# A hybrid decoder trunk's mixer entry: x turned by products with its factors' diagonal, and a quarter of its squares moved to VectorE

## The chip, the cores and the metric

The kernel runs on one core of one Trainium2 chip. The metric is the device time of one execution in microseconds (us), as the median of the runs. A separate execution was recorded by the hardware profiler; its rows name the engines PE (TensorE matmul), PEld (TensorE weight load), DVE (VectorE), ACT (ScalarE), POOL (GpSimd) and SP (SyncE).

## The reference, cut to what matters

Two layers on x of 256 tokens by 2048 features, float32: a Mamba-2 mixer and an MLP, then a differential attention on shared keys and values and a second MLP. The change touches only the first lines of the first layer:

```python
def rms_norm(x, w, eps=NORM_EPS):
    xf = x.astype(jnp.float32)
    y = xf * lax.rsqrt(jnp.mean(xf * xf, axis=-1, keepdims=True) + eps)
    return (y * w.astype(jnp.float32)).astype(x.dtype)

# layer 0
u = rms_norm(h, norm_pre_mix[l])          # h is x
zxbcdt = u @ in_proj                      # 2048 -> 10304 features
```

So each token's row of x is multiplied by one factor, the inverse root of its mean square, then each feature by its weight, and the result goes into a product with `in_proj`.

## The kernel before

**Layout.** x lies in `h` as two token halves (t = 0, 1) of 128 rows by 2048 features. It is loaded in four quarters of 512 features (`piece(0)` to `piece(3)`), one DMA each for both halves, in the SP queue (L457). The products need x with its features on the partitions, so TensorE turns it: sixteen 128-feature tiles k, each for both halves, 32 turns of 128x128 in all. A "pair" i is the tiles 2i and 2i+1, that is four turns.

**Split numbers.** Every product with a weight matrix is made of three products of rounded parts: a value is high + low, and high x high, high x low and low x high are added. Weights arrive in slabs of 128x1024 (`raw`). ScalarE makes the high part (`split`, L664), VectorE the low part (`split`, L993). The turned x, multiplied by the norm's weight `par`, is split in the same manner: ScalarE makes `xhi` out of PSUM (L680), VectorE `xlo` (L1104).

**The entry.** What happens before the first product with a weight, in the order of the code:

- ScalarE squares and sums the eight blocks (four quarters, two halves) of x as they land (`square_sum`, L667: one pass of 128x512 with an accumulator, then a read of the accumulator), and counts each in the semaphore `h_sq`.
- TensorE runs unneeded transposes of the identity, `keep_awake` (L1779): ten when `h_sq` is 4, thirteen more when it is 6 (`FIRST_AWAKE`).
- When `h_sq` is 8, VectorE adds up the sums (L1039); ScalarE takes the root (L746) after it has copied the norm weights (L758); VectorE makes the factor `rsh` of each token (L1041 to L1049).
- x is multiplied by its factors into `y`: VectorE the first 512 features (L1275, four instructions of 128x256), ScalarE the other 1536 later (`scale_x`, L767, six of 128x512), placed between its splits.
- TensorE turns `y` against the identity (`transpose_scaled_x`, L1716), which waits for the `x_scaled` semaphore of its part. Pairs 0 and 1 come first, then four more `keep_awake` transposes, then slab 0's products in three groups of eight (`high_first`: L1729, L1735, L1738). Pairs 2 and 3 are turned inside slab 1's step, pairs 4 and 5 ahead of slab 3, pairs 6 and 7 ahead of slab 4. From slab 4 on, products run in threes (L1615, L1616, L1617); slab 5 is the time step's (L1684, L1685) and needs all of x.

Each engine takes its instructions in this written order, and semaphores hold them. `diagonal` (L1054) exists in the kernel for later norms: it writes the identity times the factors into `diag`, two 128x128 tiles, which TensorE multiplies by `ones` to spread the factors (L1785). The scratch `junk` receives the squares nobody reads.

Of the kernel before, what the change touches and what calls it, by code (L numbers as in the profile page):

```python
# [25 lines left out]
ALU = mybir.AluOpType  # L26
ACT = mybir.ActivationFunctionType
AX = mybir.AxisListType.X

P = 128  # L30
D = 2048
S = 256
MT = S // P
# [19 lines left out]
PIECES = 4  # L53
# [14 lines left out]
TURN_BANKS = (((3, 3), (4, 4), (5, 5), (6, 6), (2, 2), (7, 7), (3, 3), (4, 4)), MLP_TURNS,  # L68
              ((5, 7), (6, 6), (2, 2), (7, 7), (5, 5), (6, 6), (2, 2), (7, 7)), MLP_TURNS)
# [4 lines left out]
             (1, 0, 0, 512), (1, 1, 0, 512), (1, 2, 0, 512), (1, 3, 0, 256), (1, 3, 256, 512))  # L74
END_PART_BANKS = (0, 1, 2, 3, 4, 5, 6, 7, 0)
END_AWAKE = 14
X_PIECES = ((0, 256), (256, 512), (512, 1024), (1024, 1536), (1536, 2048))
X_PIECE = (0, 1, 2, 2, 3, 3, 4, 4)
H_PIECES = ((0, 128), (128, 256), (256, 512), (512, 1024), (1024, 1536), (1536, 2048))
H_PIECE = ((0, 1), (2, 2), (3, 3), (3, 3), (4, 4), (4, 4), (5, 5), (5, 5))  # L80
LAST_PARTS = ((0, 0, 512), (1, 0, 256), (1, 256, 512))
# [116 lines left out]
def piece(n):  # L198

    return slice(n * D // PIECES, (n + 1) * D // PIECES)  # L200

def build(nc, w, out):
# [47 lines left out]
    with ctx:  # L251
        def sb(name, shape, dt=F32, stack=ctx):
            return stack.enter_context(nc.sbuf_tensor(name, shape, dt))
# [15 lines left out]
        def sem(name):  # L269
            return ctx.enter_context(nc.semaphore(name))  # L270

        h = sb("h", [P, MT, D])
        y = sb("y", [P, MT, D])
# [16 lines left out]
        def raw_of(s):  # L290
# [6 lines left out]
        junk = sb("junk", [P, 2 * MT, BLK], BF16)  # L297
        ident = sb("ident", [P, P])
# [4 lines left out]
        diag = sb("diag", [P, MT, P])  # L303

        part = sb("part", [P, MT, NT + 2 + PIECES])
        ssy, ssh = part[:, :, 0:NT + 1], part[:, :, NT + 2:]
# [3 lines left out]
        sum_y, sum_h, rsy, rsh, ssg, rsg, rsa, rs_x, rs_h, rs_a, rs_k, root = (  # L310
            stat[:, 2 * i:2 * i + 2] for i in range(12))
        neglam = sb("neglam", [P, 4])
        rs_q = sb("rs_q", [P, MT])
        ps = ctx.enter_context(nc.psum_tensor("ps", [P, 8, BLK], F32))
# [67 lines left out]
        hi_ready, lo_ready, slab_used = sem("hi_ready"), sem("lo_ready"), sem("slab_used")  # L382
        consts_ready, small_in, norm_in = sem("consts_ready"), sem("small_in"), sem("norm_in")
        x_in = [sem(f"x_in{n}") for n in range(PIECES)]
        x_scaled = [sem(f"x_scaled{n}") for n in range(len(X_PIECES))]
        heads_in, rel_in, lam_in = sem("heads_in"), sem("rel_in"), sem("lam_in")
        par_t, par_ready = sem("par_t"), sem("par_ready")
        postw_in, cum_out, cumb_in, bias_out, tab_in = (
# [3 lines left out]
        y_sq, yw_ready, h_new, h_sq, rms_ready = sem("y_sq"), sem("yw_ready"), sem("h_new"), sem("h_sq"), sem("rms_ready")  # L392
# [260 lines left out]
        def _(act):  # L653
            chain = Tally(act, act_chain)
            sc = nc.scalar

            def split(s, lo=0):

                act.wait_ge(raw_in[s.raw], s.arrived)
                if isinstance(s.n, int) and s.n >= FIRST_HELD:  # L660
                    act.wait_ge(slab_used, s.n - 2 * LEAD + 1)
                elif above(s.n, LEAD - 1):
                    act.wait_ge(slab_used, s.n - LEAD + 1)
                sc.activation(slot_of(s, lo)[0], raw_of(s), ACT.Copy).then_inc(hi_ready, 1)  # L664

            def square_sum(slot, src, dst, done):
                sc.activation(junk[:, slot, 0:src.shape[-1]], src, ACT.Square, accum_out=dst).then_inc(done, 1)  # L667

            def h_squares(r, p):

                act.wait_ge(h_new, H_STEPS * (r - 1) + MT * (p + 3))
                if p >= 2:
                    act.wait_ge(h_sq, MT * PIECES * r + MT * (p - 1))
                for t in range(MT):
                    square_sum(MT * (p % 2) + t, h[:, t, piece(p)], ssh[:, t, p:p + 1], h_sq)
# [36 lines left out]
            def output_norm(ph, r, i):  # L712

                added = NT * (ph.block0 + ph.blocks - 1)
                if i == 1:
                    root_table()
                for nt in {2: (0,), 4: (1,), 6: (2,)}.get(i, ()):
                    act.wait_ge(acc_added, added + nt + 1)
                    for t in range(MT):  # L720
                        square_sum(MT * (nt % 2) + t, y[:, t, nt * BLK:(nt + 1) * BLK], ssy[:, t, nt:nt + 1], y_sq)
                if i < 7:
                    return
                for n, (t, lo, hi) in enumerate(LAST_PARTS):
                    if n < 2:
                        act.wait_ge(part_added, 2 * r + n + 1)
                    else:
                        act.wait_ge(acc_added, added + NT)
                    sc.activation(junk[:, MT + t, lo:hi], y[:, t, (NT - 1) * BLK + lo:(NT - 1) * BLK + hi], ACT.Square,
                                  accum_out=ssy[:, t, NT - 1 + n // 2:NT + n // 2]).then_inc(y_sq, 1)  # L730
                take_root(sum_y, r + 2)
# [19 lines left out]
            for p in range(PIECES):  # L751
                act.wait_ge(x_in[p], 16)
                if p >= 2:
                    act.wait_ge(h_sq, MT * (p - 1))
                for t in range(MT):
                    square_sum(MT * (p % 2) + t, h[:, t, piece(p)], ssh[:, t, p:p + 1], h_sq)
            act.wait_ge(par_t, 1)
            sc.activation(par[:, 0:32], ps[:, 2, 0:32], ACT.Copy).then_inc(par_ready, 1)  # L758
            take_root(sum_h, 1)
            act.wait_ge(par_ready, 1)  # L760

            def scale_x(n):

                lo, hi = X_PIECES[n]
                act.wait_ge(x_scaled[1], MT)
                for t in range(MT):
                    sc.activation(y[:, t, lo:hi], h[:, t, lo:hi], ACT.Copy, scale=rsh[:, t:t + 1]).then_inc(x_scaled[n], 1)  # L767

            split(mix.slab(0))
            x_halves(0, (0, 1), 0)  # L770
            split(mix.slab(1))
            scale_x(2)
            split(mix.slab(2))
            x_halves(0, (2, 3), 0)
            split(mix.slab(3))
            scale_x(3)
            scale_x(4)

            def first_step(unit, i):

# [204 lines left out]
        def _(dve):  # L985
            chain = Tally(dve, dve_chain)
            ve = nc.vector
# [48 lines left out]
            def inverse_by_root(dst, total, sums, count, halves=range(MT)):  # L1036

                ts = slice(halves[0], halves[-1] + 1)
                ve.reduce_sum(total[:, ts], sums[:, ts, :], AX).then_inc(summed, 1)  # L1039
                dve.wait_ge(summed, count)  # L1040
                chain.mark(ve.tensor_scalar(rs_h[:, ts], total[:, ts], -0.5 / D, None, ALU.mult))  # L1041
                dve.wait_ge(rooted, count)
                link(ve.reciprocal(rs_x[:, ts], root[:, ts]))
                for t in halves:
                    c = slice(t, t + 1)
                    chain.mark(ve.scalar_tensor_tensor(out=rs_a[:, c], in0=rs_x[:, c], scalar=rs_h[:, c], in1=rs_x[:, c],
                                                       op0=ALU.mult, op1=ALU.mult))
                chain.wait()
                link(ve.scalar_tensor_tensor(out=dst[:, ts], in0=rs_a[:, ts], scalar=1.5, in1=rs_x[:, ts], op0=ALU.add, op1=ALU.mult))  # L1049
# [217 lines left out]
            ve.memset(part[:, :, NT + 1:NT + 2], 1e-6 * D).then_inc(rows_cleared, 1)  # L1267
            ve.memset(par_rows[:, :, :], 0.0).then_inc(rows_cleared, 1)
            dve.wait_ge(rows_cleared, 1)
            dve.wait_ge(h_sq, MT * PIECES)  # L1270
            inverse_by_root(rsh, sum_h, ssh_and_eps, 1)
            for n in range(2):
                lo, hi = X_PIECES[n]
                for t in range(MT):
                    ve.tensor_scalar(y[:, t, lo:hi], h[:, t, lo:hi], rsh[:, t:t + 1], None, ALU.mult).then_inc(x_scaled[n], 1)  # L1275
            dve.wait_ge(par_ready, 1)
            split(mix.slab(0))
            x_halves(0, (0, 1), 0)
# [330 lines left out]
        def _(pe):  # L1609
            te = nc.tensor  # L1610
# [96 lines left out]

            def transpose_scaled_x(i):

                pe.wait_ge(x_scaled[X_PIECE[i]], MT)  # L1710
                if i >= 6:
                    pe.wait_ge(x_lo, i - 5)
                for j in range(2):
                    for t in range(MT):
                        k = 2 * i + j
                        last = te.transpose(ps[:, TURN_BANKS[0][i][j], j * S + t * P:j * S + (t + 1) * P], y[:, t, k * P:(k + 1) * P],  # L1716
                                            ident[:, :])
                last.then_inc(xt_done, 1)

            def high_first(s, i, turns=()):  # L1720
# [368 lines left out]
            for n, (bank, lo, hi) in enumerate(END_TURNED):  # L2089
                pe.wait_ge(end_weighed, 5 + n)  # L2090
                te.matmul(ps[:, bank, 0:hi - lo], diag[:, 1, :], y[:, 1, lo:hi], start=False, stop=True,
                          skip_group_check=True).then_inc(end_done, 1)
# [21 lines left out]
```

## Time and profile before

| what | value |
|---|---|
| median of 3 runs | 2521.24 us (2520.97 to 2521.31) |
| profiled execution, its own time | 2520.59 us |
| its span on the core | 2518.6 us |
| TensorE busy | 2504.8 us (99%) |
| VectorE busy | 1821.3 us (72%) |
| ScalarE busy | 1247.8 us (50%) |
| granted TensorE clock | 1.00 up to the last microseconds |

Times of rows are counted from the span's start; the span is 1.99 us shorter than that execution's time. A busy TensorE is not TensorE at its peak, since matmuls overlap: one of 128x128 is shown with some 0.27 us, but the next may start 0.11 us later. The chain of waits shows the second figure, the distance from one to the next, and that is what a further matmul costs.

### The profile page before, as it was taken

To read this page: it belongs to the slowest core of one execution; us is meant where nothing else is said; L and a number is where in the kernel's file an instruction comes from. 1 tells how busy PE (TensorE), PEld (TensorE's weight loads), DVE (VectorE), ACT (ScalarE), POOL (GpSimd) and SP (SyncE) were. 2 spreads that over 40 slices of the span, in tenths; PEclk is the share of its full clock that TensorE was granted. 3 is DMA by queue.
4 is the path that set the end of the run, shared out by engine and by line. 5 is a ranking of instruction groups with operands and counts; after the bars stand their busy time and mean duration, and the time that the engine had idled before them with its cause. 6 is when DMAs were issued, how large, how long until landed. Compare 5 with 4: busy or idle time off the path is not lost.

```text
span 2518.6 us, 42151 instructions
## 1 busy us (share of the span) xinstructions
PE 2504.8 (99%) x15444; PEld 2237.5 (89%) x15444; DVE 1821.3 (72%) x2572; ACT 1247.8 (50%) x1631; POOL 155.9 (6%) x271
## 2 busy tenths in 40 slices
PE   8999999999999999999999999999999999999999
PEld 8999999999898888888888998998898888888887
DVE  6877877787876675766667877778866667576667
ACT  7555545555654444444444754455644444444444
POOL 2222112211100000000000000000000000000000
PEclk9999999999999999999999999999999999999999
DMA  7666566656556666666666555555566666666664
GB/s 221 214 193 205 170 191 193 200 167 201 168 192 193 184 199 189 188 190 190 192 184 199 193 176 181 179 172 168 183 189 191 192 183 197 188 191 191 191 192 151
DMA packets 267240, 474.10 MB, mean 188 GB/s; under 512 B 16673, under 2 KB 50066, under 8 KB 265618
## 3 DMA queue, kind: packets, MB, share of 16 engines
q1 hardware_dynamic: 264194, 457.53, 59.4%
q0 software_dynamic: 2624, 15.00, 1.6%
q8 instruction: 55, 0.90, 0.2%
q10 hardware_dynamic: 336, 0.41, 0.0%
q14 instruction: 31, 0.25, 0.0%
HBM read 470.70 MB, written 2.19 MB: 188 GB/s over the span
## 4 chain that ended last, share of the span: by engine, by line
PE 99%; DVE 0%; DMA 0%; issue 0%; ACT 0%; SPq 0%; ACTq 0%; DVEq 0%
PE ps L1615 23%; PE ps L1617 23%; PE ps L1616 23%; PE ps L1644 16%; PE ps L1646 9%; PE ps L1877 1%; PE ps L1751 0%; PE ps L1975 0%; PE ps L1882 0%; PE ps L1810 0%; PE ps L1779 0%; DMA h<-x 0%; PE ps L2005 0%; PE ps L1729 0%; PE ps L1716 0%
## 5 line engine op out<-in xcount | busy, mean ns | idle before, releaser
L993 DVE TENSOR_TENSOR whl<-raw,whl 128x1024 fp32r<-128x1024 f32 x856 | 1062.4, 1241 | 591.5 <-ACT whl L664 578.7
L664 ACT ACTIVATE whl<-raw 128x1024 fp32r<-128x1024 f32 x856 | 906.8, 1059 | 1084.9 <-PE ps L1617 733.8
L1644 PE MATMUL ps<-xhl,whl 128*128 128x512 f32 x1792 | 623.0, 390 | 0.0
L1646 PE MATMUL ps<-xhl,whl 128*128 128x256 f32 x1792 | 505.3, 282 | 0.0
L1615 PE MATMUL ps<-whl,bhl 128*128 128x512 f32 x1284 | 500.5, 390 | 0.0
L1617 PE MATMUL ps<-whl,bhl 128*128 128x512 f32 x1284 | 499.2, 389 | 0.0
L1616 PE MATMUL ps<-whl,bhl 128*128 128x512 f32 x1284 | 499.1, 389 | 0.0
L1615 PE MATMUL ps<-xhl,whl 128*128 128x256 f32 x1748 | 493.5, 282 | 0.0
L1616 PE MATMUL ps<-xhl,whl 128*128 128x256 f32 x1748 | 488.1, 279 | 0.0
L1617 PE MATMUL ps<-xhl,whl 128*128 128x256 f32 x1748 | 487.6, 279 | 0.0
L1644 PEld LDWEIGHTS ps<-xhl,whl 128*128 128x128 f32 x1792 | 336.4, 188 | 71.1
L1646 PEld LDWEIGHTS ps<-xhl,whl 128*128 128x128 f32 x1792 | 338.6, 189 | 1.1
L1615 PEld LDWEIGHTS ps<-xhl,whl 128*128 128x128 f32 x1748 | 328.6, 188 | 0.5
L1616 PEld LDWEIGHTS ps<-xhl,whl 128*128 128x128 f32 x1748 | 328.8, 188 | 0.1
L1617 PEld LDWEIGHTS ps<-xhl,whl 128*128 128x128 f32 x1748 | 328.5, 188 | 0.0
L1615 PEld LDWEIGHTS ps<-whl,bhl 128*128 128x128 f32 x1284 | 241.0, 188 | 54.0 <-issue 4.8
L1617 PEld LDWEIGHTS ps<-whl,bhl 128*128 128x128 f32 x1284 | 241.1, 188 | 50.1
L1616 PEld LDWEIGHTS ps<-whl,bhl 128*128 128x128 f32 x1284 | 241.2, 188 | 47.8
L1093 DVE TENSOR_TENSOR y<-y,ps 128x1024 f32<-128x1024 f32 x138 | 168.4, 1220 | 5.1 <-PE ps L1617 0.8
L1615 PE MATMUL ps<-khl,whl 128*128 128x256 f32 x256 | 72.6, 284 | 0.0
L1617 PE MATMUL ps<-khl,whl 128*128 128x256 f32 x256 | 71.5, 279 | 0.0
L1616 PE MATMUL ps<-khl,whl 128*128 128x256 f32 x256 | 71.5, 279 | 0.0
(268 smaller groups left out, 2082.0 us busy)
## 6 DMA issues: line engine op xcount, KB each, us to landing
raw<-mlp_w SPq DMA_DIRECT2D x512, 512.0 KB, 4.2
raw<-a_in_proj SPq DMA_DIRECT2D x161, 512.0 KB, 4.6
raw<-a_out_proj SPq DMA_DIRECT2D x64, 512.0 KB, 4.1
raw<-b_w_q SPq DMA_DIRECT2D x32, 512.0 KB, 4.2
raw<-w_k SPq DMA_DIRECT2D x32, 512.0 KB, 4.1
raw<-w_v SPq DMA_DIRECT2D x32, 512.0 KB, 3.7
raw<-b_out_proj SPq DMA_DIRECT2D x32, 512.0 KB, 3.7
cumb<-cum_scratch POOLq DMA_DIRECT2D x8, 1024.0 KB, 7.2
```

The lines of the kernel that those rows point to most:

```text
L664: sc.activation(slot_of(s, lo)[0], raw_of(s), ACT.Copy).then_inc(hi_ready, 1)
L993: ve.tensor_tensor(out=low, in0=raw_of(s), in1=hi.bitcast(F32), op=ALU.subtract).then_inc(lo_ready, 1)
L1093: ve.tensor_tensor(out=cols, in0=cols, in1=ps[:, bank:bank + 2, :], op=ALU.add).then_inc(acc_added, 1)
L1615: te.matmul(outs, lh, rh, start=start, stop=False, skip_group_check=True)
L1616: te.matmul(outs, lh, rl, start=False, stop=False, skip_group_check=True)
L1617: return te.matmul(outs, ll, rh, start=False, stop=stop, skip_group_check=True)
L1644: te.matmul(ps[:, f, :].rearrange("p (q n) -> p q n", q=2), wh[:, j, c], xboth[:, :, k, :], start=k == 0, stop=False, skip_group_check=True)
L1646: last = te.matmul(ps[:, f, 0:S], wl[:, j, c], xhi[:, k, :], start=False, stop=k == KT - 1, skip_group_check=True)
L1877: te.matmul(ps[r % 2 * PD:(r % 2 + 1) * PD, 5 + r // 4, col:col + P], xd[:, c, r * PD:(r + 1) * PD], m[:, c, r, :], start=True, stop=True, ...
```

## The change

- The scaling of x goes away on both engines (L767 and L1275), with its semaphores `x_scaled`.
- In its place VectorE writes the factors on a diagonal with `diagonal(rsh, x_diag)`, two instructions of 128x128.
- TensorE turns unscaled x: the block of `h` is the stationary operand, `diag[:, t, :]` the moving one, so that the product is the turned block times the factors. It is an ordinary float32 `matmul`, no longer a `transpose`. All 32 wait for one semaphore, `x_diag`.
- The squares of the second token half of quarters 2 and 3 go from ScalarE to VectorE (`tensor_tensor_reduce`). ScalarE's one remaining square of each of these quarters counts two in `h_sq`.

```diff
-            def square_sum(slot, src, dst, done):
-                sc.activation(junk[:, slot, 0:src.shape[-1]], src, ACT.Square, accum_out=dst).then_inc(done, 1)
+            def square_sum(slot, src, dst, done, counts=1):
+                sc.activation(junk[:, slot, 0:src.shape[-1]], src, ACT.Square, accum_out=dst).then_inc(done, counts)
...
-                for t in range(MT):
-                    square_sum(MT * (p % 2) + t, h[:, t, piece(p)], ssh[:, t, p:p + 1], h_sq)
+                for t in range(MT if p < 2 else 1):
+                    square_sum(MT * (p % 2) + t, h[:, t, piece(p)], ssh[:, t, p:p + 1], h_sq, 1 if p < 2 else MT)
...
-            def scale_x(n):
-
-                lo, hi = X_PIECES[n]
-                act.wait_ge(x_scaled[1], MT)
-                for t in range(MT):
-                    sc.activation(y[:, t, lo:hi], h[:, t, lo:hi], ACT.Copy, scale=rsh[:, t:t + 1]).then_inc(x_scaled[n], 1)
-
             split(mix.slab(0))
             x_halves(0, (0, 1), 0)
             split(mix.slab(1))
-            scale_x(2)
             split(mix.slab(2))
             x_halves(0, (2, 3), 0)
             split(mix.slab(3))
-            scale_x(3)
-            scale_x(4)
...
             dve.wait_ge(rows_cleared, 1)
+            for p in range(2, PIECES):
+                dve.wait_ge(x_in[p], 16)
+                dve.wait_ge(h_sq, MT * (p - 1))
+                chain.mark(ve.tensor_tensor_reduce(
+                    out=junk[:, MT * (p % 2) + 1, :], in0=h[:, 1, piece(p)], in1=h[:, 1, piece(p)], scale=1.0, scalar=0.0,
+                    op0=ALU.mult, op1=ALU.add, accum_out=ssh[:, 1, p:p + 1]))
+            chain.wait()
             dve.wait_ge(h_sq, MT * PIECES)
             inverse_by_root(rsh, sum_h, ssh_and_eps, 1)
-            for n in range(2):
-                lo, hi = X_PIECES[n]
-                for t in range(MT):
-                    ve.tensor_scalar(y[:, t, lo:hi], h[:, t, lo:hi], rsh[:, t:t + 1], None, ALU.mult).then_inc(x_scaled[n], 1)
+            diagonal(rsh, x_diag)
...
             def transpose_scaled_x(i):
 
-                pe.wait_ge(x_scaled[X_PIECE[i]], MT)
+                if i == 0:
+                    pe.wait_ge(x_diag, MT)
                 if i >= 6:
                     pe.wait_ge(x_lo, i - 5)
                 for j in range(2):
                     for t in range(MT):
                         k = 2 * i + j
-                        last = te.transpose(ps[:, TURN_BANKS[0][i][j], j * S + t * P:j * S + (t + 1) * P], y[:, t, k * P:(k + 1) * P],
-                                            ident[:, :])
+                        last = te.matmul(ps[:, TURN_BANKS[0][i][j], j * S + t * P:j * S + (t + 1) * P], h[:, t, k * P:(k + 1) * P],
+                                         diag[:, t, :], start=True, stop=True, skip_group_check=True)
                 last.then_inc(xt_done, 1)
```

The order of instructions at the places that matter. TensorE, from the first fillers (`ident` alone is a `keep_awake` transpose) to slab 0's first products, before:

```order
L1779 MATMUL ps<-ident 128x128 x9
L1779 MATMUL ps<-ident 128x128 [waits h_sq]
L1779 MATMUL ps<-ident 128x128 x12
L1716 MATMUL ps<-ident,y 128x128 [waits x_scaled0]
L1716 MATMUL ps<-ident,y 128x128 x3
L1716 MATMUL ps<-ident,y 128x128 [waits x_scaled1]
L1716 MATMUL ps<-ident,y 128x128 x3
L1779 MATMUL ps<-ident 128x128 x4
L1729 MATMUL ps<-xhl,whl 128x256 [waits x_hi,hi_ready]
```

The same stretch of TensorE after, where lines of this part of the file have numbers 7 lower:

```order
L1772 MATMUL ps<-ident 128x128 x12
L1709 MATMUL ps<-diag,h 128x128 [waits x_diag]
L1709 MATMUL ps<-diag,h 128x128 x7
L1772 MATMUL ps<-ident 128x128 x4
L1722 MATMUL ps<-xhl,whl 128x256 [waits x_hi,hi_ready]
```

The eight turns stay where they were, between the 23 fillers and the four; two waits have become one. The order counts instructions of the program, one for each product, whatever it is on the engine.

VectorE, from the cleared rows to slab 0's low part, before (`stat` holds the sums, the root and the factors):

```order
L1268 MEMSET par_rows 128x512
L1039 TENSOR_REDUCE stat<-part 128x2 [waits h_sq,rows_cleared]
L1041 TENSOR_SCALAR stat<-stat 128x2 [waits summed]
L1043 RECIPROCAL stat<-stat 128x2 [waits rooted]
L1046 SCALAR_TENSOR_TENSOR stat<-stat 128x1 [waits dve_chain]
L1046 SCALAR_TENSOR_TENSOR stat<-stat 128x1
L1049 SCALAR_TENSOR_TENSOR stat<-stat 128x2 [waits dve_chain]
L1275 TENSOR_SCALAR y<-h,stat 128x256 [waits dve_chain]
L1275 TENSOR_SCALAR y<-h,stat 128x256 x3
L993 TENSOR_TENSOR whl<-raw,whl 128x1024 [waits hi_ready,par_ready]
```

The same stretch after, with line numbers 12 lower behind the squares:

```order
L1256 MEMSET par_rows 128x512
L1261 ISA junk,part<-h 128x512 [waits h_sq,x_in2,rows_cleared]
L1261 ISA part 128x1
L1261 ISA junk,part<-h 128x512 [waits h_sq,x_in3]
L1261 ISA part 128x1
L1027 TENSOR_REDUCE stat<-part 128x2 [waits h_sq,dve_chain]
L1029 TENSOR_SCALAR stat<-stat 128x2 [waits summed]
L1031 RECIPROCAL stat<-stat 128x2 [waits rooted]
L1037 SCALAR_TENSOR_TENSOR stat<-stat 128x2 [waits dve_chain]
L1042 TENSOR_SCALAR diag<-ident,stat 128x128 [waits dve_chain]
L1042 TENSOR_SCALAR diag<-ident,stat 128x128
L981 TENSOR_TENSOR whl<-raw,whl 128x1024 [waits hi_ready,par_ready]
```

Each square on VectorE is two instructions (the pass and the read of its sum), and both stand ahead of the first sum of sums. The four scalings have become two writes of the diagonal.

## Rows read from the trace of the kernel before

**Rows 1.** The page: busy time of each engine.

```profile
PE 2504.8 (99%) x15444; PEld 2237.5 (89%) x15444; DVE 1821.3 (72%) x2572; ACT 1247.8 (50%) x1631; POOL 155.9 (6%) x271
```

**Rows 2.** Stretches: from:to and length us, TensorE busy (records), granted clock, DMA share, GB/s.

```profile
8.43:12.82 4.39, 4.38 (x23) 1.00 1.06 401
13.18:31.00 17.82, 17.76 (x151) 1.00 0.84 206
31.00:60.00 29.00, 29.00 (x252) 1.00 0.64 194
...
100.00:2505.00 2405.00, 2403.72 (x14610) 1.00 0.61 187
```

**Rows 3.** The chain of waits, first 16 us: start us, us, what.

```profile
1.95 6.52 DMA h<-x
...
9.85 1.34 ACT junk L667 x4
...
11.29 0.17 DVE stat L1039
...
12.51 0.19 DVE y L1275
12.70 0.08 issue
12.77 0.36 DVE y L1275
13.13 0.04 issue
13.18 1.18 PE ps L1716 x8
14.36 0.44 PE ps L1779 x4
14.79 0.06 issue
14.85 1.18 PE ps L1729 x8
```

**Rows 4.** The queries on x: issue of quarters 2 and 3, and their landing.

```profile
L457 SPq DMA_DIRECT2D h<-x x2: 463/502/541, 2.0 to 2.5; - x2
...
DMA to landing us min/median/max: 6.5/6.9/7.4
```

**Rows 5.** Timeline, entry: start us, us, engine, line, operation [idle before, releaser].

```profile
9.85 0.63 ACT L667 ACTIVATE junk<-h 128x512 bf16<-128x512 f32 x1
...
10.39 0.18 ACT L667 ACTIVATION_READ_ACCUMULATOR junk<-h 128x1 f32 x1
...
13.87 1.57 ACT L680 ACTIVATE xhl<-ps,par 128x256 fp32r<-128x256 f32 x4 [1.23 <-PE ps L1716]
```

**Rows 6.** Timeline of TensorE's fillers, from 8 and from 12.5 us.

```profile
8.43 3.46 PE L1779 MATMUL ps<-ident 128*128 128x128 f32 x15 [1.18 <-ACT junk L667]
...
12.32 0.49 PE L1779 MATMUL ps<-ident 128*128 128x128 f32 x3
```

**Rows 7.** Instruction groups with forms kept apart: xcount, busy us, mean ns, idle before.

```profile
L1716 PE MATMUL ps<-ident,y 128*128 128x128 f32 x32 | 4.3, 276 | 0.4 <-DVE y L1275 0.4
L1785 PE MATMUL ps<-diag,ones 128*128 128x128 f32 x12 | 1.8, 274 | 0.0
L1054 DVE TENSOR_SCALAR diag<-ident,stat 128x128 f32<-128x128 f32 x6 | 3.0, 540 | 0.0
L1450 DVE SCALAR_TENSOR_TENSOR relu<-relu,rs_row 128x512 f32<-128x512 f32 x56 | 36.2, 688 | 1.0
L1161 DVE SCALAR_TENSOR_TENSOR h<-y,stat,h 128x512 f32<-128x512 f32 x18 | 12.7, 745 | 0.1
L1049 DVE SCALAR_TENSOR_TENSOR stat<-stat 128x2 f32<-128x2 f32 x4 | 0.6, 160 | 0.1
```

**Rows 8.** The chain of waits at three later places.

```profile
24.38 0.87 PE ps L1716 x8
...
82.47 1.09 PE ps L1882 x8
...
729.15 0.44 PE ps L1785 x4
```

**Rows 9.** The diagonals of later norms: count, ns min/median/max.

```profile
L1054 DVE TENSOR_SCALAR diag<-ident,stat x6: 278/285/1057, 722.6 to 1832.0; 128x128 f32<-128x128 f32 x6
```

More of the change, by code:

```diff
@@ L76 @@
 END_AWAKE = 14
-X_PIECES = ((0, 256), (256, 512), (512, 1024), (1024, 1536), (1536, 2048))
-X_PIECE = (0, 1, 2, 2, 3, 3, 4, 4)
 H_PIECES = ((0, 128), (128, 256), (256, 512), (512, 1024), (1024, 1536), (1536, 2048))
@@ L384, in build @@
         x_in = [sem(f"x_in{n}") for n in range(PIECES)]
-        x_scaled = [sem(f"x_scaled{n}") for n in range(len(X_PIECES))]
+        x_diag = sem("x_diag")
         heads_in, rel_in, lam_in = sem("heads_in"), sem("rel_in"), sem("lam_in")
```

## The prediction

> **What bounds the kernel now.** I read the page's busy line first: TensorE is busy for 2504.8 of 2518.6 us, and no other engine is above three quarters [rows 1]. So the 13.8 us in which it isn't busy are looked for next, in the stretches: from 31 to 60 us it is busy all the time, and in the 2405 us from 100 on it lacks 1.28 us [rows 2]. What is left lies ahead of the first products, and in the tail, which the change doesn't touch. Two rules follow. Whatever is added to TensorE's own queue behind the entry is paid in full. Whatever is taken from ScalarE or VectorE behind the entry is worth nothing, because they don't hold TensorE there.
>
> The entry itself is read in the chain of waits [rows 3]: x's third quarter lands at 8.47, ScalarE squares until 11.19, the factors take until 12.5, two scalings of VectorE until 13.13, and TensorE turns from 13.18, fills with four transposes, and starts slab 0's products at 14.85. From there the chain is TensorE alone. So the question is when the products with slab 0 start, and how much is added behind.
>
> **The squares.** ScalarE's four passes between x's third quarter, at 8.5, and 11.19 become two [rows 3]. But the last quarter bounds the gain: it was issued at 2.5 and took 7.4 us to land, so it is there at about 9.9 [rows 4]. ScalarE's last remaining square can't start earlier than the one that starts at 9.85 now, and its accumulator is read by 10.39 + 0.18 = 10.57 [rows 5]. VectorE's square has no row here. Its nearest are passes of 128x512 over two float32 operands, 0.688 to 0.745 us, and 0.16 us for an operation on one or two columns, as the read of the sum is [rows 7]. With 0.70 + 0.16, less some overlap, from 9.9 it ends at 10.7, and the sum of sums starts at about 10.8, where it started at 11.29 [rows 3]. Gain: 0.5 us, not the 1.3 us that ScalarE sheds. Bounds: nothing gained below the landing (ScalarE's 10.57, so at best 0.6 us), and on the other side a pass at half that rate, below.
>
> **The diagonal.** Before, the first scaling started 12.51 - 11.29 = 1.22 us behind the sum of sums, and the second ended 0.62 us later [rows 3]. Now the first diagonal write starts at 10.8 + 1.22 = 12.02. Two writes of 128x128, 0.28 us each in most of the six rows there are and 0.2 us apart, end at 12.4. The longest of the six took 1.06 us [rows 9]; that is the upper bound, and would make it 13.3. I take 0.28, the median.
>
> **What the earlier factors meet.** TensorE is not free at 12.4. Its 23 fillers start at 8.43, when ScalarE has squared quarter 1, which the change leaves where it is. Fifteen of them are (3.46 - 0.48) / 14 = 0.213 us apart, the last ones 0.11 us, and the last starts at 12.54 [rows 6], so the next instruction can start at 12.65. The second group of fillers waits for `h_sq` of 6, which is reached earlier now, but the first ten last until 8.43 + 10 x 0.213 = 10.56 anyway, so nothing moves. The turns start at 12.65 instead of 13.18: 0.53 us.
>
> **The turns.** This is the term that decides. A turn was a transpose: 32 in the program, 32 records, eight in 0.87 us, 0.109 each [rows 7, 8]. Now it is a float32 product. The kernel has the like: `spread_rs` multiplies `ones` by `diag`, two products for each of three norms, six in all, and the trace has twelve records of them, four in 0.44 us [rows 7, 8]. So a float32 product of 128x128 is two records of 0.11, and a turn goes from 0.109 to 0.218 us. A dearer neighbour is L1882 (four products for a group, eight records): 1.09 us, 0.136 each, with waits in it [rows 8]. I take 0.109, since the nearest shape is the diagonal's own.
>
> - Pairs 0 and 1: 8 x 0.218 = 1.74, from 12.65 to 14.39; then four fillers, 0.44, to 14.83; slab 0's products follow at 14.85 to 14.9. That is the time they start at now. Is the other input there? ScalarE starts on the turned pair 0.69 us behind the first turn, and needs some 0.8 us for two tiles [rows 5]; a pair takes 0.44 us longer now, so 12.65 + 1.13 + 0.8 = 14.6. Yes, just. VectorE, free from 12.4 and with two writes for four scalings, has slab 0's low part earlier. So the 0.53 us gained ahead of the turns are spent in them: net zero.
> - Pairs 2 to 7: 24 turns stand between products in a queue without gaps, so each costs its whole 0.109 more: 24 x 0.109 = 2.6 us. Their readers have room: ScalarE's and VectorE's parts of pair 7 take under 3 us behind the last turn, (four tiles take ScalarE 1.57 us [rows 5]), beside slab 4's 24 products at the 29.0 / 252 = 0.115 us of a record in rows 2, 2.8 us, and slab 5, which needs them, comes after.
>
> **The scalings.** ScalarE loses six passes and VectorE four. Nothing waited for ScalarE's, and by the first rule this is worth nothing. It is cover, though, for ScalarE's part of the turned x and slab 4's split, which come earlier against TensorE. No queue of SP or POOL is passed by anything.
>
> **The sum.** 0 at the start, +2.6 behind it. The profiled span goes from 2518.6 to 2521.2, its time from 2520.59 to 2523.2; against the median of the runs, 2521.24, that is 2523.9 us, 0.10% more. A measurement of this kernel can tell about 0.2%, 5.0 us, from no change, so the call is "the same", with a leaning to slower. Up to 1.3 us of it could be taken up by the short gaps behind 100 us [rows 2]; at the dearer 0.136 the 48 records of pairs 2 to 7 cost 6.5 us where the 24 transposes cost 2.6, so +3.9: 2525.1.
>
> **Rivals.**
>
> - *VectorE comes late.* If its square takes twice the 0.69 us of the nearest pass, 1.38, the first one runs from 8.5 past 9.9, the second to 11.3, with the read 11.45, behind ScalarE's end of today. Then the diagonal is there at 13.1, and everything is 0.45 us later: 2524.4. A diagonal write of 1.06 us gives 0.65 us in its own right, both together 1.3: up to 2525.2. For it: neither has a clean row in the entry. Against it: every pass of two float32 operands in rows 7 runs at the single rate. Chance 0.14. The Trainium skill (Vector Engine (DVE) Microarchitecture Reference, Points that are easy to get wrong) says that a scalar-tensor-tensor shape with two sources in SBUF that aren't bf16 runs at half throughput, no port being left for the accumulator. By that rule the rival would hold for the square; rows 7 disagree for the same shape without an accumulator (L1161, 745 ns), and no row shows one with it.
> - *The other side: a product is four records.* Slower than before by more than 0.2%. If TensorE took a real float32 product against a data block in four records, a turn would cost 0.436: pairs 0 and 1 end at 12.65 + 3.49 = 16.14, slab 0 starts at 16.6, 1.75 late, and the others add 24 x 0.327 = 7.85: 2530.8. It decides from three records a turn on: 24 x 2 x 0.109 + 0.9 = 6.1 us, beyond 5. Against it: twelve records for six products [rows 7]. Chance 0.04. The Trainium skill (TensorE: Matmul & The Clock Gate, Terms) names the transpose mode as four times faster for FP32; by that rule this rival would be the result. The trace says two.
> - *A turn stays one record.* If the product cost what the transpose did, pairs 0 and 1 would be done at 13.52, ScalarE's first tiles at about 14.15, and slab 0 would start 0.65 us earlier: 2520.6. Against it stand the same twelve records. Chance 0.04.
> - *The change doesn't bring its factors earlier*, because the last quarter lands late and the fillers end late. That is part of the forecast for the half it is true.
>
> **How the numbers follow.** Forecast, with its small variations, 0.74: 2523.9. VectorE late 0.14: 2524.4 to 2525.2. Four records 0.04, one record 0.04, and 0.04 for something in the placement of the program that rows don't show, either side. The first two hold 0.88, so the range goes from the forecast less the gaps' 1.3 and the run's own spread, 2522.0, to the dearer price on top with a late diagonal, 2526.0. Above 2526.3 (slower by over 0.2%) lie the four-record case and half of the rest: 0.06. Faster by over 0.2% would need 5 us from an entry in which 0.65 is the most that I find: 0.01. The same: 0.93.
>
> **What the changed profile would show.** The turns as 64 records, eight products (16 records) in 1.74 us in the chain; if there are 32 or 128, the sum fails. The sum of sums at 10.8 (11.45: half rate). The first turn at 12.65 with the last filler just ahead of it; if it starts at 13.1 or later with "DVE diag" as its releaser, VectorE is late. Slab 0's first product between 14.8 and 15.0. ScalarE idle more from 16 to 28 us, TensorE without a gap there, and its products from slab 4 on starting 2.6 us later than now. The forecast is wrong if a gap opens ahead of slab 4 or 5, or if the span from the first product on changes by other than 2.6 us.

## The result

| | before | changed |
|---|---|---|
| median | 2521.10 us (2520.79 to 2522.17, 22 runs) | 2524.27 us (2523.77 to 2525.59, 22 runs) |
| profiled execution's span | 2518.6 us | 2522.1 us |
| median span of those runs | 2519.1 us | 2522.35 us |

The ratio is 1.0012, with a 95% interval of 1.0007 to 1.0018: 3.2 us more, inside the 0.2% that count as no change here, and with the sign that the sum gave. The forecast was 2523.9, so 2.7 or 2.8 us more. The 3.5 us between the two profiled spans is a little too much: the span of before in its profile is 0.5 us shorter than its median span. Where this lies is said below.

### The profile page after: what moved, and what is told of

It is laid out like the page before. It is cut to its first block, busy times and chain, and to the rows that moved or that the text cites. A ratio compares the mean times of both kernels' runs of the same rounds, so it can differ in the third digit from the quotient of the medians.

```text
span 2522.1 us, 42207 instructions
## 1 busy us (share of the span) xinstructions
PE 2508.2 (99%) x15476; PEld 2241.0 (89%) x15476; DVE 1823.0 (72%) x2574; ACT 1243.7 (49%) x1621; POOL 156.4 (6%) x271
## 4 chain that ended last, share of the span: by engine, by line
PE 98%; DVE 1%; DMA 0%; ACT 0%; issue 0%; SPq 0%; ACTq 0%; DVEq 0%
PE ps L1607 23%; PE ps L1609 23%; PE ps L1608 23%; PE ps L1636 16%; PE ps L1638 9%; PE ps L1870 1%; PE ps L1744 0%; DVE whl L981 0%; PE ps L1968 0%; PE ps L1875 0%; PE ps L1803 0%; PE ps L1709 0%; DMA h<-x 0%; PE ps L1772 0%; DVE y L1081 0%
```

## The profile after

Line numbers are those of the changed kernel: 7 lower for TensorE, 12 for VectorE, 2 for ScalarE. First the page's busy line, which answers to [rows 1]:

```profile
PE 2508.2 (99%) x15476; PEld 2241.0 (89%) x15476; DVE 1823.0 (72%) x2574; ACT 1243.7 (49%) x1621; POOL 156.4 (6%) x271
```

TensorE has 15476 - 15444 = 32 records and 3.4 us of busy time more; ScalarE is 4.1 us less busy. Where the records are, by the query on the line of the turns (count, ns min/median/max, first and last start):

```profile
L1709 PEld LDWEIGHTS ps<-diag,h x64: 186/192/193, 12.9 to 31.6; 128*128 128x128 f32 x64
L1709 PE MATMUL ps<-diag,h x64: 270/275/377, 12.9 to 31.7; 128*128 128x128 f32 x64
```

32 turns are 64 records where they were 32 in [rows 7]. Now the chain of waits, to be laid beside [rows 3] (start us, us, what):

```profile
2.46 7.23 DMA h<-x
...
10.31 0.73 ACT junk L665 x2
...
11.14 0.18 DVE stat L1027
...
12.36 0.55 DVE diag L1042 x2
...
12.95 2.05 PE ps L1709 x16
15.00 0.44 PE ps L1772 x4
15.44 0.93 PE ps L1722 x8
...
19.17 1.78 PE ps L1709 x16
...
25.63 1.79 PE ps L1709 x16
...
30.21 1.78 PE ps L1709 x16
```

Two things are to be seen. Behind the first product with a weight each group of eight turns takes 1.78 or 1.79 us where it took 0.87: 5.35 - 2.61 = 2.74 us in three groups. One of the three groups of before is in [rows 8]; the other two are:

```profile
18.83 0.87 PE ps L1716 x8
...
28.07 0.87 PE ps L1716 x8
```

Ahead of it, slab 0's products start later. How much has to be read from the timelines of TensorE. The chain gives an instruction that waited its real start (14.85 before), but one that followed another on the same engine the modelled end of that other (15.44 now). The real starts, before and then now:

```profile
14.19 0.60 PE L1779 MATMUL ps<-ident 128*128 128x128 f32 x4
14.85 1.18 PE L1729 MATMUL ps<-xhl,whl 128*128 128x256 f32 x8
```

```profile
12.95 2.05 PE L1709 MATMUL ps<-diag,h 128*128 128x128 f32 x16 [0.69 <-DVE diag L1042]
14.84 0.60 PE L1772 MATMUL ps<-ident 128*128 128x128 f32 x4
15.19 1.18 PE L1722 MATMUL ps<-xhl,whl 128*128 128x256 f32 x8
```

So slab 0's products start 15.19 - 14.85 = 0.34 us late, where the forecast had zero. The turns started 0.23 us earlier than before (12.95 against 13.18), they took 1.89 us instead of 1.01 up to the first of the four fillers, and from there to the products it is 0.35 us instead of 0.66, since TensorE waited there before.

The sum of sums was only 0.15 us earlier than before (11.14 against 11.29), since the last quarter landed later in this execution. Its landing can be read off VectorE's square, for which everything else was done by 9.7:

```profile
10.27 0.69 DVE L1261 CUSTOM_DVE_ANT_0 junk<-h 128x512 bf16<-128x512 f32 x1 [0.54 <-DMA h<-x]
10.31 0.63 ACT L665 ACTIVATE junk<-h 128x512 bf16<-128x512 f32 x1 [0.63 <-issue]
...
10.88 0.08 DVE L1261 DVE_READ_ACCUMULATOR2_ANT part<- 128x1 f32 x1
```

It landed at some 10.3 us, against 9.9 in [rows 4]. (The chain's row for x ends at 9.69, where ScalarE had finished its square before; the query on x's transfers gives up to 7.8 us from issue to landing, and 2.46 + 7.8 is 10.3.) The square takes 0.69 us and the read of its sum 0.08. From landing to the sum of sums it is 0.85 us now; before, ScalarE alone took from 9.85 to 11.29, 1.44 us. So that part is worth its 0.6 us at this place. Behind the entry TensorE is as busy as before: 2403.7 us of the 2405 from 100 us on (2403.72 before, 2403.65 after).

```profile
100.00:2505.00 2405.00, 2403.65 (x14620) 1.00 0.61 187
```

The start and the turns make 0.34 + 2.74 = 3.1 us of the 3.5 between the two profiled spans. The rest need not be the change's. From slab 0's first product to the end, the execution of before took 2518.6 - 14.85 = 2503.8 us. Five other profiles below that also have single transposes behind the first pairs took 2504.0 to 2504.4, and those with products for all turns 2506.7 to 2507.1. The profile of before is the shortest of its kind by 0.2 to 0.6 us.

## The experiments

All medians are of 11 executions, each beside the kernel before on the same chip (33 executions). The intervals of the ratios are all about 0.09% wide to either side, that is 2.3 us. They separate the group at 3 us from zero, but not differences of a few tenths, which I read from the medians and from the profiles together and call indications.

### One part alone: the squares

```diff
-                for t in range(MT):
-                    square_sum(MT * (p % 2) + t, h[:, t, piece(p)], ssh[:, t, p:p + 1], h_sq)
+                for t in range(MT if p < 2 else 1):
+                    square_sum(MT * (p % 2) + t, h[:, t, piece(p)], ssh[:, t, p:p + 1], h_sq, 1 if p < 2 else MT)
...
+            for p in range(2, PIECES):
...
+                chain.mark(ve.tensor_tensor_reduce(
```

> The kernel before with the squares' part of the change alone: VectorE squares the second token half of quarters 2 and 3, the scaling of x and the transposes stay. My theory (the squares' part brings the factors half a microsecond earlier, TensorE's added records cost the rest): about 0.45 us faster than before, 2520.65 us, with the first turn some 0.45 us earlier than in a before whose last quarter lands at the same time. Rival (the fillers or the landing hold the turns whatever the squares do): no change, 2521.1 us. Rival (the squares on VectorE cost time): over 2521.3 us.

Measured: 2520.95 us against 2521.20, ratio 0.9998 (0.9989 to 1.0007). Not to be told from no change, and half of the 0.45 us expected. Its profile shows why the other half may be missing. The fillers, the factors' last scalings and the turns (timeline):

```profile
8.44 5.12 PE L1786 MATMUL ps<-ident 128*128 128x128 f32 x23 [1.18 <-ACT junk L667]
...
12.38 1.14 DVE L1282 TENSOR_SCALAR y<-h,stat 128x256 f32<-128x256 f32 x4
13.40 1.04 PE L1723 MATMUL ps<-ident,y 128*128 128x128 f32 x8
```

The second of the four scalings ends at about 13.0, but the turns start at 13.40: the 23 fillers took 5.12 us, all 0.213 us apart, where those of before took 4.38 (the first fifteen 0.213 apart, the last ones 0.11 [rows 6]). Here the fillers hold the turns.

### One part undone: the squares back on ScalarE

```diff
-                for t in range(MT if p < 2 else 1):
-                    square_sum(MT * (p % 2) + t, h[:, t, piece(p)], ssh[:, t, p:p + 1], h_sq, 1 if p < 2 else MT)
+                for t in range(MT):
+                    square_sum(MT * (p % 2) + t, h[:, t, piece(p)], ssh[:, t, p:p + 1], h_sq)
...
-            for p in range(2, PIECES):
...
-                chain.mark(ve.tensor_tensor_reduce(
```

> The changed kernel with all eight squares back on ScalarE, so that only the diagonal and the products are left of the change. My theory: the 24 later turns cost 2.7 us, the first eight 0.9 us less what the two shorter writes of the diagonal give back (0.2 us): about 3.4 to 3.6 us slower than before, 2524.6 us, so 0.3 to 0.45 us slower than the changed kernel. Rival (the squares on VectorE are a cost of the change and not a gain): as fast as the changed kernel or faster, 2524.3 us or less.

Measured: 2524.06 us against 2521.20, ratio 1.0011 (1.0002 to 1.0020). The loss is here without the squares' part. But it is 2.9 us, less than the 3.4 to 3.6 expected. So it was run once more, in a later job beside the changed kernel:

> The changed kernel with the squares back on ScalarE, once more, on one chip with the changed kernel. My theory of the forecast (the squares' part gains half a microsecond ahead of the turns): 0.3 us or more slower than the changed kernel. Theory after the first job (inside the change the squares' part gains nothing, since the fillers, whose end varies, and not the factors let TensorE go): within 0.15 us of it.

> The changed kernel itself once more, on the chip of this job, as the measure for the others: 3.0 us slower than before, 2524.2 us.

Measured: products only 2523.81, changed 2524.01, before 2521.06 us (ratios 1.0011, 1.0002 to 1.0020; and 1.0012, 1.0003 to 1.0021). The squares' part, which alone gave an indication of 0.25 us, shows no gain inside the change. Two things can be seen behind it. One is the fillers again; the chains of the two profiles, products only and then the changed kernel:

```profile
8.50 5.17 PE ps L1765 x23
13.67 1.95 PE ps L1702 x16
```

```profile
8.38 4.84 PE ps L1772 x23
13.22 1.79 PE ps L1709 x16
```

In both the chain goes from the fillers straight to the turns; neither the squares nor the diagonal are in it. In the changed kernel the second write of the diagonal had ended at 12.10 + 0.54 = 12.64, and the turns started behind the last filler, at 13.05 in the timeline. This isn't so in every execution. In the first profiles of the same two programs both chains go through the squares and the diagonal: the turns start at 13.37 with products only and at 12.95 in the changed kernel, though x's last quarter was squared from 10.16 in the one and from 10.31 in the other. There the squares' part did bring the turns forward. How often it does, no run counts; the median spans say little on average. The other is outside the span: the median span is 2522.2 us for products only and 2522.1 for the changed kernel, but the execution's time is 1.64 us longer than the span for products only, 1.92 for the changed kernel and 1.97 for before. In the first job it was 1.62 as well, and the changed kernel with early fillers, below, has 1.78. Why the time around the span differs between programs isn't known; no row shows it.

### The later turns as transposes again

```diff
-                        last = te.matmul(ps[:, TURN_BANKS[0][i][j], j * S + t * P:j * S + (t + 1) * P], h[:, t, k * P:(k + 1) * P],
-                                         diag[:, t, :], start=True, stop=True, skip_group_check=True)
+                        dst, c = ps[:, TURN_BANKS[0][i][j], j * S + t * P:j * S + (t + 1) * P], slice(k * P, (k + 1) * P)
+                        if i < 2:
+                            last = te.matmul(dst, h[:, t, c], diag[:, t, :], start=True, stop=True, skip_group_check=True)
+                        else:
+                            last = te.transpose(dst, y[:, t, c], ident[:, :])
```

ScalarE's `scale_x` comes back with it, and waits for `x_diag`.

> The changed kernel for the squares, the diagonal and pairs 0 and 1, but ScalarE scales the other 1536 features of x again and pairs 2 to 7 are transposes of the scaled x, as before. My theory (24 products of two records each cost 24 x 0.11 us more than 24 transposes): 2.65 to 2.75 us faster than the changed kernel, 2521.6 us, so 0.3 to 0.6 us slower than before. Rival (the loss comes from the entry, where TensorE waits for the diagonal): at most 0.5 us faster than the changed kernel, 2523.8 us or more.

Measured: 2521.52 us against 2521.20, ratio 1.0002 (0.9993 to 1.0011). All but 0.3 us of the loss is gone (2.75 us against the changed kernel's 2524.27), with the squares, the diagonal and the first eight products still in. From the chain:

```profile
18.96 0.87 PE ps L1728 x8
...
24.51 0.87 PE ps L1728 x8
...
28.19 0.87 PE ps L1728 x8
```

The three groups are back at 0.87 us. The loss sits in pairs 2 to 7, and ScalarE's six scalings beside them cost nothing.

### Records without products

Before, with each of these 24 transposes issued twice into the same place:

```diff
-                        last = te.transpose(ps[:, TURN_BANKS[0][i][j], j * S + t * P:j * S + (t + 1) * P], y[:, t, k * P:(k + 1) * P],
-                                            ident[:, :])
+                        for again in range(1 if i < 2 else 2):
+                            last = te.transpose(ps[:, TURN_BANKS[0][i][j], j * S + t * P:j * S + (t + 1) * P],
+                                                y[:, t, k * P:(k + 1) * P], ident[:, :])
```

> The kernel before, with each of the 24 transposes of pairs 2 to 7 issued twice into the same place; nothing else of the change. My theory (what the change costs is the number of records in TensorE's queue behind the first product, whatever they compute): 24 x 0.11 = 2.6 us slower than before, 2523.8 us. Rival (a record of a float32 product is dearer than a transpose, or the loss is elsewhere): clearly less than the 2.85 us by which the transposes from pair 2 on were faster than the changed kernel, under 2 us. Rival (TensorE's queue has room here): no change.

Measured: 2523.88 us against 2521.03, ratio 1.0010 (1.0001 to 1.0019): 2.85 us. From the chain:

```profile
19.64 1.75 PE ps L1717 x16
...
26.06 1.75 PE ps L1717 x16
```

Sixteen transposes take 1.75 us, sixteen records of products 1.78. So what is paid is a record's place in TensorE's queue; that it is a product and not a transpose makes 0.03 us for sixteen. Within what the medians can tell this is the change's whole later loss, without a diagonal, without a float32 product and without any of its other parts.

### The four fillers between turns and products

```diff
-AWAKE, FIRST_AWAKE = 24, (10, 13, 4)
+AWAKE, FIRST_AWAKE = 24, (10, 13, 0)
```

> The changed kernel without the four unneeded transposes between the first turns and slab 0's products. My theory: in the changed kernel's profile these products start straight behind the fillers (15.19 behind 14.84 plus 0.44), and ScalarE's first two tiles of the turned x are ready at about 15.0, so 0.2 to 0.3 us is gained: 2524.0 us. Rival (ScalarE's tiles end the wait by themselves and the fillers lie beside it): no change, 2524.3 us.

Measured: 2524.21 us against 2521.20, ratio 1.0011 (1.0002 to 1.0020): 3.01 us more than before, where the changed kernel has 3.17 and 2.95. These medians can't tell my 0.2 to 0.3 us from nothing. The profile speaks for the rival, no change. Timeline:

```profile
14.30 2.03 PE L1709 MATMUL ps<-diag,h 128*128 128x128 f32 x16
...
15.47 1.73 ACT L678 ACTIVATE xhl<-ps,par 128x256 fp32r<-128x256 f32 x4 [1.42 <-PE ps L1709]
...
16.46 0.71 PE L1722 MATMUL ps<-xhl,whl 128*128 128x256 f32 x4
```

ScalarE's first two tiles, 0.8 to 0.9 us from 15.47, end at 16.3, and the product starts at 16.46 without fillers in between. From the first turn to the product it is 2.16 us, against 2.24 and 2.15 in the two profiles of the changed kernel. Turns and fillers together only just cover these tiles; when the fillers go, the tiles are the wait.

### The fillers ahead of the turns: earlier, or fewer

Seven more fillers, begun when `h_sq` is 2 (squares-only, changed and before with this alone):

```diff
+            pe.wait_ge(h_sq, MT)
+            keep_awake(7, 0)
             for n in range(2):
```

> The squares-only kernel with seven more fillers, started two squares earlier (at about 6.8 us instead of 8.4). My theory (in many executions the fillers still run 0.21 us apart when the factors are there, so that they and not the factors let TensorE go at 13.3; TensorE comes up to its full rate the earlier the earlier it is kept busy): fillers end before 12.5, the first turn follows VectorE's second scaling, 0.2 us faster than squares-only, 2520.7 us. Rival (the fillers don't hold the turns): the same as squares-only, 2520.95 us. Rival (seven more transposes are just work in the way): slower than squares-only.

> The changed kernel with the same seven early fillers. My theory: 0.2 to 0.4 us faster than the changed kernel (2524.2), the first turn starting straight behind the second write of the diagonal, and still 2.7 us slower than the squares-only kernel with early fillers. Rival (the diagonal, not the fillers, holds the turns in most executions): no change, 2524.2 us.

> The kernel before with the seven early fillers alone. My theory: its factors come late enough for the fillers to be done in most executions, so at most 0.1 us faster than before, 2521.1 us. Rival (the fillers hold the kernel before as well): 0.2 us or more faster, as much as the early fillers give the squares-only kernel.

Measured against 2521.03: 2520.90 (0.9999, 0.9990 to 1.0008), 2523.92 (1.0011, 1.0002 to 1.0020) and 2521.12 (1.0000, 0.9991 to 1.0009). None differs from its kernel without these fillers by more than the measurement can tell. The mechanism that I had put behind the first two is refuted by the profiles. The fillers of squares-only, of changed and of before:

```profile
7.09 6.37 PE L1786 MATMUL ps<-ident 128*128 128x128 f32 x30
```

```profile
7.08 6.30 PE L1772 MATMUL ps<-ident 128*128 128x128 f32 x30
```

```profile
7.13 6.29 PE L1779 MATMUL ps<-ident 128*128 128x128 f32 x30
```

Thirty at 0.213 us are 29 x 0.213 + 0.27 = 6.4 us: nearly all ran at the wide spacing, although TensorE had been kept busy 1.3 us longer. Being busy earlier didn't bring the narrow spacing forward (it came at 13.0, 12.9 and 12.9), and the additional fillers ended no sooner: turns at 13.30, 13.22 and 13.41.

Five fillers less:

```diff
-AWAKE, FIRST_AWAKE = 24, (10, 13, 4)
+AWAKE, FIRST_AWAKE = 24, (10, 8, 4)
```

> The squares-only kernel with five fillers less ahead of the turns (18 for 23). In the profiles so far TensorE went over from 0.21 to 0.11 us a filler between 11.1 and 14.4 us, whatever time they began at. My theory (the fillers' end holds the turns where that comes late): at 0.213 us each the 18 end at 12.3, the turns start with the factors at 12.7, 0.2 to 0.3 us faster than squares-only, 2520.7 us. Rival (the gap ahead of the turns, or turns that run at the slower spacing, give it back): 2520.95 us or more.

> The changed kernel with five fillers less ahead of the turns. My theory: where the fillers' end holds the turns, 0.2 to 0.4 us faster than the changed kernel of the same job. Rival (16 records at the slower spacing, 0.21 us each, take longer than the fillers did): the same or up to 0.5 us slower.

Measured against 2521.06: squares-only 2520.69 us (0.9999, 0.9990 to 1.0008), changed 2523.94 (1.0013, 1.0004 to 1.0022). Squares-only with 18 fillers has the lowest median of all kernels here, 0.37 us below before, where 23 fillers gave 0.25; the changed kernel gains 0.07 at most, which is nothing. The timeline of the first:

```profile
8.23 3.53 PE L1786 MATMUL ps<-ident 128*128 128x128 f32 x18 [1.16 <-ACT junk L667]
...
12.97 1.18 PE L1723 MATMUL ps<-ident,y 128*128 128x128 f32 x8 [1.21 <-DVE y L1282]
```

TensorE is idle for 1.21 us ahead of the turns, and they run at the narrow spacing all the same. The direction agrees with the fillers as the holder, and the size is too small to be shown. This profile doesn't show it either: the narrow spacing came at 11.0 in it, as early as in the changed kernel's first profile, where all 23 fillers were through by 12.1. No version beats before by more than the measurement can tell.

## Why the prediction was right, point by point

- **TensorE is the bound; behind the entry its queue is paid in full.** Held. 24 idle transposes cost 2.85 us, 24 second records of the changed kernel 2.74 us in the chain. The 1.3 us of gaps behind 100 us took up nothing; they were there unchanged.
- **A turn becomes two records.** Held: 64. The term was 24 x 0.109 = 2.6; it measured 2.74 in the chain, because sixteen records of products take 1.78 us, 0.111 each, and not 1.74. The rivals of four records and of one are refuted by the count. The rule of the Trainium skill (TensorE: Matmul & The Clock Gate, Terms), a transpose mode four times as fast for FP32, doesn't hold here: eight turns take 1.78 us as products and 0.87 as transposes, a factor of two.
- **The squares: 0.5 us.** The durations held: 0.69 + 0.08 us where 0.70 + 0.16 had been put, and from the landing to the sum of sums 0.6 us less than before. The rival of half rate is refuted. The rule of the Trainium skill (Vector Engine (DVE) Microarchitecture Reference, Points that are easy to get wrong), half throughput for want of a port for the accumulator, would have made the pass 1.38 us; the trace disagrees for this operation, which it names CUSTOM_DVE_ANT_0 and not a scalar-tensor-tensor. What failed is the time at which it starts. I had taken the landing at 9.9 us from one execution as fixed, and it moves: the first square of the last quarter starts between 9.85 and 11.64 us in the profiles here.
- **The diagonal.** Two writes in 0.50 to 0.55 us, not the 0.4 that I had from 12.02 to 12.4, and not 1.06 each. A small miss, in part of arithmetic: 0.28 us each and 0.2 apart make 0.48.
- **The start of slab 0's products: no change.** This is the term that was mis-sized: 0.34 us late in the profiled execution, not 0. The step that failed is the start of the turns at 12.65: "the last filler starts at 12.54 [rows 6], so the next instruction can start at 12.65", with the diagonal there at 12.4. Both were one execution's figures. In the changed kernel's profile the fillers were done by 12.1, but the diagonal came at 12.91, since x had landed 0.4 us later and the writes took 0.55 us; the turns started at 12.95. In its second profile the diagonal was there at 12.64 and the fillers held until 13.05. The 23 fillers took 4.1 to 5.3 us in the profiles, depending on when TensorE goes over to the narrow spacing, and the turns started between 12.7 and 13.5 us in all profiles but two, in which x landed late (13.98 and 14.30), with or without earlier factors. The turns' own length held: 1.89 us instead of 1.01, the 0.87 more that the forecast had, and so did the slack behind them, 0.31 us where 0.87 - 0.53 = 0.34 were counted on. What was missing is 0.3 us of the 0.53 by which the turns were to start earlier.
- **The sum.** 0.34 + 2.74 gives 3.1 us: the median spans differ by 3.0 and 3.25 in the two jobs, the times by 2.95 and 3.17. The range, 2522.0 to 2526.0, held both. That the start could miss by a third of a microsecond without harm is because the later turns, which were sized rightly, make nine tenths of the sum. That a gain and a cost at the start would cancel to the tenth was a coincidence of one profile's times.
- **The scalings are worth nothing.** Held: with ScalarE's six back, and the transposes with them, the loss was gone.

What stays open: why the program with the products alone has 0.3 us less around its span; whether the squares' part is worth its 0.25 to 0.37 us alone, since no interval here excludes zero; and how often the fillers and how often the factors let the turns go, since each run left one profile.

## What to carry to other kernels

Ask of every rewrite on the busiest engine how many records it makes and read that count from the trace, not from the program: a float32 product of this shape is one instruction in the code and two records on TensorE, so folding a scaling into a transpose doubles the transpose on the one engine that has no room, to save work on two that have. A time of one profile is a draw as soon as a DMA's landing or a rate that changes stands ahead of it; where a sum uses "starts at 12.65", look at how much the event ahead of it moves between executions. And work that only fills time is an instruction in the queue like any other: it can be what the next step waits for.

## What the runs showed of the hardware that I had not expected

- VectorE's multiply-and-sum over 512 float32 elements takes 0.69 us and 0.08 for its result, ScalarE's square and sum of the same block 0.63 and 0.19.
- A transpose and a record of a float32 product, both of 128x128, cost the same place in the queue: sixteen in 1.75 and in 1.78 us.
